# Hybrid decoder step: gate columns projected inside attention, VectorE order in attention and the selection of the late PEER heads rearranged

## What is computed

```python
z = rmsnorm(x, norm_mix) @ w_in              # q, six k/v parts, nsa gates, ssm input u, 2048 merge gates g_mrg
o = gates_cmp*attn_cmp + gates_sel*attn_sel + gates_win*attn_win     # 8 heads of 64, prompt: causal over <=512 keys
y = s5_scan(u)                               # diagonal complex state space, 2048 states
m = sigmoid(g_mrg[:, :1024]) * (o @ w_att_proj) + sigmoid(g_mrg[:, 1024:]) * glu(gelu(y) @ w_ssm_glu)
x = x + m @ w_out
# PEER: 8 heads, 2 x 128 product keys, top 16 of each half, top 16 of the 256 sums
v1, i1 = top_k(q1 @ k1.T, 16); v2, i2 = top_k(q2 @ k2.T, 16); sc, ci = top_k(v1 + v2, 16); e = i1*128 + i2
x = x + sum_hk softmax(sc) * gelu(u_tab[e] . h) * v_tab[e]           # 128 experts for each token
```

## Time and profile before

| | us |
|---|---|
| median of 3 runs | 2407.54 |
| profiled execution, its own time | 2404.02 |
| its span | 2402.3 |
| TensorE busy in the span | 1781.3 (74%) |
| VectorE busy | 1387.7 (58%) |
| GpSimd busy | 685.8 (29%) |
| ScalarE busy | 300.2 (12%) |
| mean granted TensorE clock | 0.772 |
| bytes moved by DMA | 653.88 MB, 562.07 MB of them by GpSimd's gathers |

### The profile page before, as it was taken

How to read it: one execution, slowest core, us unless ns; L and a number is a source line. 1 busy time by engine, 2 the same in 40 slices (tenths; PEclk the granted TensorE clock), 3 DMA queues, 4 the chain that set the end, 5 groups by cost and what they waited for, 6 DMA issues and landing times.

```text
span 2402.3 us, 22802 instructions
## 1 busy us (share of the span) xinstructions
PE 1781.3 (74%) x7910; PEld 814.7 (34%) x7910; DVE 1387.7 (58%) x3448; ACT 300.2 (12%) x686; POOL 685.8 (29%) x828
## 2 busy tenths in 40 slices
PE   7998859997779873888876678656666666666666
PEld 6444746653348561544431334201101011101111
DVE  3899214541132174788645576796577744677644
ACT  3000212220110120222111110000000000000000
POOL 4920100005210202332333222333333333333331
PEclk9899958997999995998986687756665656665557
DMA  4011450005333327999999799899999999999996
GB/s 161 0 50 41 106 157 1 1 1 153 95 103 132 126 79 272 420 414 410 411 414 411 292 382 362 331 359 410 415 416 421 404 415 412 413 410 407 416 413 256
DMA packets 129743, 653.88 MB, mean 272 GB/s; under 512 B 22068, under 2 KB 37092, under 8 KB 59932
## 3 DMA queue, kind: packets, MB, share of 16 engines
q0 software_dynamic: 80000, 562.07, 58.5%
q1 hardware_dynamic: 49628, 90.34, 10.8%
HBM read 645.29 MB, written 11.26 MB: 273 GB/s over the span
## 4 chain that ended last, share of the span: by engine, by line
DMA 22%; PE 17%; DVE 12%; issue 8%; POOL 3%; ACT 0%; DVEq 0%; POOLq 0%; SPq 0%; ACTq 0%
DMA ex_uv<-in_peer_uv,idxT 21%; PE ex_acc L2039 9%; DVE ex_uv L2160 4%; PE ex_hb L1942 3%; POOL ex_uv L1835 3%; DVE ch_iu L1531 1%; PE ex_late L1964 1%; DVE ch_v L1528 1%; PE ex_pick L1992 1%; DVE ch_ci L1531 1%; PE ex_pick L2023 1%; DVE ch_sc L1528 1%; PE ex_late L1992 1%; DVE ch_s L1535 1%; PE ex_late L1979 1%
## 5 line engine op out<-in xcount | busy, mean ns | idle before, releaser
L2160 DVE SCALAR_TENSOR_TENSOR ex_uv<-ex_uv,ex_hb 128x1024 f32<-128x1024 f32 x520 | 628.4, 1219 | 415.8 <-DMA ex_uv<-in_peer_uv,idxT 318.9
L1835 POOL DMA_INDIRECT ex_uv<-in_peer_uv,idxT x520 | 493.0, 948 | 1027.5 <-PE ex_acc L2039 836.3
L1942 PE MATMUL ex_hb<-ex_h_rows,spread 24*128 24x512 bf16 x1040 | 355.8, 505 | 440.3 <-DVE ex_uv L2160 416.8
L2039 PE MATMUL ex_acc<-ex_uv,wts 128*32 128x512 f32 x2080 | 437.3, 963 | 0.0
L1942 PEld LDWEIGHTS ex_hb<-ex_h_rows,spread 24*128 24x128 bf16 x1040 | 52.9, 99 | 775.2 <-DVE ex_uv L2160 629.0
L2275 ACT ACTIVATE ex_gelu<-ex_dots 128x4 f32<-128x4 f32 x130 | 26.7, 205 | 1118.2 <-DVE ex_uv L2160 1116.0
L2039 PEld LDWEIGHTS ex_acc<-ex_uv,wts 128*32 128x32 f32 x2080 | 76.0, 149 | 260.3 <-issue 260.3
L515 PE MATMUL pz<-pr_hT,pr_ring 128*128 128x256 f32 x320 | 71.2, 382 | 0.3 <-ACT hx L443 0.3
L1015 POOL MEMSET de_qbd<- 128x576 f32 x1 | 0.6, 577 | 231.5 <-POOLq L99 231.5
L515 PEld LDWEIGHTS pz<-pr_hT,pr_ring 128*128 128x128 f32 x320 | 60.6, 191 | 10.3 <-issue 1.2
L1528 DVE MAX8 ch_v<-ch_s 128x8 f32<-128x128 f32 x128 | 31.1, 285 | 56.0 <-ACT ch_s L2247 50.6
(11 more groups left out here) (449 smaller groups left out, 2431.6 us busy)
## 6 DMA issues: line engine op xcount, KB each, us to landing
ex_ring<-in_late_w SPq DMA_DIRECT2D x24, 1024.0 KB
pr_ring<-in_w_in SPq DMA_DIRECT2D x6, 2048.0 KB, 8.1
ex_uv<-in_peer_uv,idxT POOLq DMA_INDIRECT x520
w_q<-in_peer_w_q SPq DMA_DIRECT2D x8, 1024.0 KB, 7.7
w_out<-in_w_out SPq DMA_DIRECT2D x2, 2048.0 KB, 17.4
ex_h_rows<-h_split SPq DMA_DIRECT2D x65, 48.0 KB
pr_x<-in_x_prompt SPq DMA_DIRECT2D x4, 512.0 KB, 5.1
pr_ring<-in_w_in_heads SPq DMA_DIRECT2D x1, 2048.0 KB, 10.4
```

Of the source, the lines that this page charges most:

```text
L1835: pool.indirect_dma_start(uv[:, s % SLOTS].rearrange("p j n -> p (j n)"), None, table, bass.IndirectOffsetOnAxis(ap=S.idxT[:, t:t + 1], ax ...
L1942: last = pe.matmul(hb[s % 2][:, CHUNK * h:CHUNK * h + CHUNK], spread[p, k % LOAD, :], h_rows[p, l % 2, CHUNK * h:CHUNK * h + CHUNK], start ...
L2039: last = pe.matmul(acc[LANE * g:LANE * g + LANE, CHUNK * h:CHUNK * h + CHUNK], wts[:, s % (2 * BATCH), LANE - 1 - r:2 * LANE - 1 - r], uv[ ...
L2160: dve.scalar_tensor_tensor(out=rows_, in0=rows_, scalar=1.0, in1=hb[s % 2][:], op0=ALU.mult, op1=ALU.mult, accum_out=dots[:, B % 2, c:c + ...
```

## The change

1. Of the four g chunks only the first stays in `stage_project`; the PE loop runs max(19, 21) = 21 steps, the gelu of the ssm output comes after all groups, cos and sin are loaded right behind the last ring load, and chunks 1 and 2 are loaded into the ring for later (`load_gates`). `hT` and the ring outlive the stage.
2. In `stage_attend` the 12 other groups run: 8 behind the q and k transposes, 2 while VectorE does the compressed softmax, 1 in each of query tiles 0 and 2 of the compressed products. Their sigmoids are on ScalarE (`keep_gates`). SyncE loads chunk 3 between the `w1` loads and the other compression weights, after 4 groups are done.
3. In the units `maxima` is split into `mask` and `maxima`. For i of 2 and 3 the copy L758 comes between them, and the first `keep_busy` is left out.
4. In `stage_experts` the late half-heads are selected in batch j + 33, for late tiles 0 and 2 (tile 2 and the samples); the scores of late tile 1 (tile 3) are kept in `s3` and selected at b = 1 to 16 of tile 2. The splits into thirds are 6 batches apart instead of 3, with `store_rows` ahead of the piece loads. `CHOOSE_LATE` goes from 16 to 17, the exchange of the choice from b = 26 to 27 for n > 0.

```diff
@@ stage_project
-        chunks += [(NAT + 512 + CHUNK * j, CHUNK, "g") for j in range(4)]
+        chunks += [(NAT + 512, CHUNK, "g")]
...
             sp.dma_start(sin, io["rope_sin"]).then_inc(E["tables"], 16)
+            load_gates(sp, io, S, 1, E["z_done"], ends[3])
...
+            load_gates(sp, io, S, 2, E["z_done"], ends[4])
...
-            for j in range(FIRST, len(groups)):
-                s = j - FIRST
+            for s in range(max(len(groups) - FIRST, len(steps) + 5)):
...
-                project(j)
+                if FIRST + s < len(groups):
+                    project(FIRST + s)
+
+def load_gates(sp, io, S, c, done, count):
+    src = io["w_in"].rearrange("a (k p) n -> p (a k) n", p=P)
+    sp.wait_ge(done, count)
+    c0 = NAT + CHUNK + CHUNK * c
+    sp.dma_start(S.ring[:, c % 2], src[:, :, c0:c0 + CHUNK]).then_inc(S.gate_w[c % 2], 16)
@@ stage_attend, SyncE
                     sp.dma_start(S.w1[HD * g:HD * g + HD, j], io[src].rearrange("a s d h -> d (a s) h")).then_inc(E["w_cmp"], 16)
+            load_gates(sp, io, S, 3, E["g_done"], 4)
@@ VectorE
-            def maxima(u):
+            def mask(u):
...
+            def maxima(u):
...
                 if u + 1 < len(UNITS):
-                    maxima(u + 1)
+                    mask(u + 1)
+                    if i < 2:
+                        maxima(u + 1)
...
                 dve.tensor_copy(probT[:, b, 1, 0:P * i + P], tp[:, 1, 0:P * i + P]).then_inc(E["pt1"], 1)
+                if i >= 2 and u + 1 < len(UNITS):
+                    maxima(u + 1)
@@ ScalarE
+            def keep_gates(n, bank):
+                act.wait_ge(E["g_done"], n + 1)
+                act.activation(S.sgT[:, 4 + n, :], bank[:, 0:EARLY_TOK], ACT.Sigmoid).then_inc(E["g_kept"], 1)
...
             act.activation(pc[:], pc[:], ACT.Exp).then_inc(E["cexp_ready"], 1)
+            for n in (8, 9):
+                keep_gates(n, tp[:, n - 8, :])
@@ TensorE
+            def gates_of(n, bank):
...
+            for n in range(8):
+                if n >= 4:
+                    pe.wait_ge(E["g_kept"], n - 3)
+                gates_of(n, sc[:, n % 4, :])
...
+            for n in (8, 9):
+                gates_of(n, tp[:, n - 8, :])
+            pe.wait_ge(E["g_kept"], 10)
             pe.wait_ge(E["coefc_ready"], 1)
...
+                if i % 2 == 0:
+                    gates_of(10 + i // 2, sc[:, i // 2, :])
                 pe.wait_ge(E["ct_kept"], i + 1)
...
-                keep_busy(tp[:, 0, :])
+                if i < 2:
+                    keep_busy(tp[:, 0, :])
@@ stage_experts
-        CHOOSE_LATE = QUERY_AT + HH + 1 - LANE
+        CHOOSE_LATE = QUERY_AT + HH + 2 - LANE
...
-            return B - QUERY_AT - 1 if 0 <= B - QUERY_AT - 1 < HH else None
+            return B - QUERY_AT - 2 if 0 <= B - QUERY_AT - 2 < HH else None
...
+                for t in range(LATE):
+                    if B == TURN_AT + 6 * t + 3:
+                        store_rows(t)
                 for p in range(2, PIECES):
...
-                for t in range(LATE):
-                    if B == TURN_AT + 3 * t + 3:
-                        store_rows(t)
...
-                    dve.wait_ge(E["s_kept"], hh + 1)
-                    best16(dve, link, [(R.v[:, EARLY + t, hh, :], R.iu[:, EARLY + t, hh, :], s2[:, hh % 2, t, :])
-                                       for t in range(TILES - EARLY)])
+                    dve.wait_ge(E["s_kept"], 2 * hh + 2)
+                    best16(dve, link, [(R.v[:, t, hh, :], R.iu[:, t, hh, :], s2[:, hh % 2, t // 2 - 1, :])
+                                       for t in (2, 4)])
...
+                if n == 2 and 1 <= b <= HH:
+                    best16(dve, link, [(R.v[:, 3, b - 1, :], R.iu[:, 3, b - 1, :], s3[:, b - 1, :])])
...
-                t, step = divmod(B - TURN_AT, 3)
+                t, step = divmod(B - TURN_AT, 6)
```

More of the change, by code:

```diff
@@ L476, in _ @@
                 keep(j)
-                if j == GELU_AT:
-                    for k in range(8):
-                        hf, u = divmod(k, 4)
-                        part = S.uT[:, u, SPAN * hf:SPAN * hf + SPAN]
-                        act.wait_ge(E["y_ready"], k + 1)
-                        act.activation(part, part, ACT.Gelu_apprx_tanh).then_inc(E["gelu_done"], 1)
-                    act.wait_ge(E["hs_kept"], 1)
-                    act.activation(S.uT[:, :, SEQ:TOK], y[:, 1, 0:4 * NB].rearrange("p (u b) -> p u b", b=NB),
-                                   ACT.Gelu_apprx_tanh).then_inc(E["gelu_done"], 1)
+            for k in range(8):
+                hf, u = divmod(k, 4)
+                part = S.uT[:, u, SPAN * hf:SPAN * hf + SPAN]
+                act.wait_ge(E["y_ready"], k + 1)
+                act.activation(part, part, ACT.Gelu_apprx_tanh).then_inc(E["gelu_done"], 1)
+            act.wait_ge(E["hs_kept"], 1)
+            act.activation(S.uT[:, :, SEQ:TOK], y[:, 1, 0:4 * NB].rearrange("p (u b) -> p u b", b=NB),
+                           ACT.Gelu_apprx_tanh).then_inc(E["gelu_done"], 1)
         @block.tensor
@@ L746, in maxima @@
                 link(dve.tensor_tensor(diag, diag, causal[:].unsqueeze(1).broadcast_to([P, 2, P]), ALU.add))
+            def maxima(u):
+                i, h = UNITS[u]
+                b = u % 2
                 link(dve.tensor_reduce(nmax[:, b, :], sc[:, 2 * b:2 * b + 2, 0:P * i + P], AX_X, ALU.max))
                 dve.tensor_scalar(nmax[:, b, :], nmax[:, b, :], -1.0, None, ALU.mult).then_inc(E["max_ready"], 1)
+            mask(0)
             maxima(0)
@@ L848, in _ @@
                 last.then_inc(E["tr_done"], 1)
+            def gates_of(n, bank):
+                c, m = divmod(n, 4)
+                c += 1
+                if m == 0:
+                    pe.wait_ge(S.gate_w[c % 2], 16 * (c // 2 + c % 2))
+                for k in range(KT):
+                    last = pe.matmul(bank[:, 0:EARLY_TOK], S.ring[:, c % 2, k, P * m:P * m + P], S.hT[:, k, :],
+                                     start=(k == 0), stop=(k == KT - 1))
+                last.then_inc(E["g_done"], 1)
+            for n in range(8):
+                if n >= 4:
+                    pe.wait_ge(E["g_kept"], n - 3)
+                gates_of(n, sc[:, n % 4, :])
             pe.wait_ge(E["tr_kept"], 2 * TILES)
@@ L867, in _ @@
             pe.wait_ge(E["cmp_kept"], 3)
+            pe.wait_ge(E["g_kept"], 8)
             for i in range(NQ):
@@ L1797, in stage_experts @@
         HH = 2 * HEADS_P
-        CHOOSE, TURN, KEEP = 3, 26, 27
-        CHOOSE_LATE = QUERY_AT + HH + 1 - LANE
+        CHOOSE = 3
+        CHOOSE_LATE = QUERY_AT + HH + 2 - LANE
+        TURN = [26 if n == 0 else 27 for n in range(TILES)]
         EXP = [CHOOSE_LATE + HEADS_P if n == 1 else CHOOSE + HH for n in range(TILES)]
@@ L2054, in _ @@
                 late_work(B, 1)
-                if n < TILES - 1 and b == TURN:
+                if n < TILES - 1 and b == TURN[n]:
                     pe.wait_ge(E["eg_ready"], n + 1)
@@ L2285, in _ @@
                     act.activation(R.eg[:, 1, :], R.eg[:, 1, :], ACT.Exp).then_inc(E["exped"], 1)
-                if n < TILES - 1 and b == KEEP:
+                if n < TILES - 1 and b == TURN[n] + 1:
                     act.wait_ge(E["eg_done"], n + 1)
@@ L2306, in build @@
                                          for n, k in (("merge", 2), ("out", 2), ("route", 4)))
+        S.gate_w = [ctx.enter_context(nc.semaphore(f"gate_w{j}")) for j in range(2)]
         S.out_gain, S.route_keys = (ctx.enter_context(nc.semaphore(n)) for n in ("out_gain", "route_keys"))
```

32 lines of the change are left out of this document (21 added, 11 removed).

## The result

The changed kernel takes 2337.05 us (median of 4 runs, 2333.22 to 2341.23), the kernel before 2407.37 on the same chip: a ratio of 0.9706, 95% interval 0.9685 to 0.9727. The profiled execution has a span of 2331.5 us against 2402.3, 70.8 less. The sum is where it was forecast; its terms are not.

A forecast was written before the change was run, and what follows sets the result against it. Bounds: a chain of waits in attention's front, TensorE's work in the units, DMA in tile 2, VectorE and store waits in tile 1. Terms sum to -70.1 us, 2404.0 to 2333.9, at the median's place 2337; range 2320 to 2360.

The forecast's parts named there:

- Projection, -28.2: End of the projection: twelve gate groups leave, rope starts near 242 instead of 267.9, attention starts about 28.2 us earlier.
- the small product then follows at once, near 241: End of the projection: with twelve groups gone, VectorE gets the small product near 241 and starts rope near 242.
- Front, +13.3: Front of attention: the moved gate groups partly fill TensorE's waits and lengthen the stretch by 13.3 us, bounds +8 and +20.
- Units, -15.4: Attention units: 16 units of i = 2 and 3 lose 0.96 us each with the first dummy, bounds -10 and -15.4.
- the products start on time: Units: VectorE's copy, now ahead of the maxima, ends by T + 1.8, before the second dummy ends at T + 1.9.
- Tile 1, -41.8: Experts, tile 1: selection and store waits go, transfers bound; 354.3 us against 396.1, bounds -50 and -30.
- The row of 28.05 us: Experts, tile 1: SyncE's queue stood 28 us in two piece loads, holding the store ScalarE awaited for 13.04 us.
- Tile 2, +2: Experts, tile 2: sixteen one-row selections of 1.84 us just fit under the transfers; 2 us for unevenness, bounds 0 and +14.
- The front gives more back: Rival, front of attention: four later groups on a cold array cost 13.8 us more, 2351 in all; chance 0.13.
- VectorE bound in tile 2: Rival, experts' tile 2: the added selection is not hidden at all, +27 us, 2364 in all; chance 0.10.
- The clock falls in the units: Rival, units: without the first dummy they run at 1.2 GHz, 83 us more, 2420 in all; chance 0.04.
- The chain in tile 1 stays: Rival, experts' tile 1: scores still awaited in their own batch, 21 us less gain, 2358 in all; chance 0.03.

The follow-up runs named there:

- gates_late: Changed kernel with gate groups 10 and 11 behind the four steps of the compressed products instead of within two of them: 2342.92 us, ratio 0.9743 to the kernel before.
- front_warm: Changed kernel with four dummy matmuls in TensorE's waits in the front of attention: 2328.53 us, ratio 0.9685 to the kernel before.
- only_two_behind: Kernel before with only the selection two batches behind its query, three rows and stores as before: 2376.49 us, ratio 0.9889.

## Why the prediction was right, point by point

**Bound of each stretch: right.** A chain in the front, TensorE's list in the units, VectorE's wait and the store in tile 1, transfers in tile 2. The experiments take the first three out one by one and find their prices; for tile 2 there is the DMA share of 1.01 in both kernels, with 209 and with 235 us of VectorE's work.

**Projection, -28.2: 4.0 too much.** The failed step is "the small product then follows at once, near 241". Twelve groups left, but four of the first chunk stay, and when the state is ready TensorE has the end of one group and the whole of the last still ahead of the product. The order of the instructions showed that before the run. With the product ahead of the last group (`small_first`) rope starts at 242.7, the forecast's place within 0.7.

**Front, +13.3: 7.9 too much, outside its bounds of +8 to +20.** Part of it held: hidden matmuls 35.9 us into the stage (38.4 forecast), no weight late, two groups beside the softmax at +1.2 (1.3 forecast). The largest failed term is the clock in the four steps. Groups 10 and 11 were to cost 4.7 less 2; the four steps took 26.4 us with them against 27.3 without, -0.9 for +2.7. Next is the start-up, put 2.5 too high: of the 4.3 us added for a cold start and a table load 1.8 came (transposes until 8.2 us into the stage, not 6.5, groups 27.7 and not 27.6). The hidden matmuls gave 2 back and not 1, and the piece up to the compressed scores 0.5. `gates_late` and `front_warm` show why: a step cost 6.62 us because its matmuls ran at the lower of the clock's two levels, 1.2 GHz, and both fillings that were tried, gate groups and dummies, paid for themselves. The lower bound +8 assumed full clock in the products and did not take what it gives: 1.91 to 1.06 and 3.67 to 1.99.

**Units, -15.4: 2.5 too much.** The failed step is "the products start on time". The copy arrives at T + 1.87, the products start at T + 2.02, so the copy is the bound of that piece. It was 1.91 before, so a unit loses 0.96 - 0.11 = 0.85 us. The last unit gained nothing (its transposes come 4.84 us after those before it, 4.64 in the kernel before); the forecast gave all sixteen the full gain. That the order is what makes the dummy removable is shown: 3.4 us without it, 12.9 with.

**Tile 1, -41.8: 3.4 too much.** The choice for tile 2 ran at 369 GB/s for 68.7 us, a loss of 68.7 x (1 - 369/413) = 7.3 us (8.1 forecast). The failed step is that this was the only loss in the sum. A second one stands from 1327 to 1370: the rate is 370, 43 x (1 - 370/413) = 4.5 us, where the second late tile's state is split and VectorE waits 3.83 us for ScalarE. That wait alone does not explain it, since the third tile's split has the same 3.83 us at 1404.87 in a stretch (1398 to 1434) that moves 419 GB/s. What delays the gathers stays open.

One reading of the forecast was loose here. The row of 28.05 us joins two piece loads whose issues take 0.36 us each, at 1329.13 and 1356.83; between them SyncE waited for a query of TensorE. The store went out at 1357.23, and ScalarE's 13.04 us are the time until it landed (1370.27); in `only_two_behind` they are 1349.81 to 1363.48. So a store needs some 13 us there, and what the change gives it is time.

**Tile 2, +2: it took 0.1.** The one-row selections, 26 us of VectorE's work (235, not 209), were hidden whole.

**Rivals.** The front gives more back: fell (5.4 us, clock 0.86). VectorE bound in tile 2: fell. The clock falls in the units: fell, even without both dummies. The chain in tile 1 stays: fell. By the Trainium skill's rule (TensorE: Matmul & The Clock Gate, "A second HAM failure mode: psum-queue depth-cycling") short idles between groups of matmuls can make the clock swing. In the units it does not (0.93 us idle in 5.9, clock 0.98). In the compressed products the trace agrees in part: with waits of 1.10 us the clock was at 0.50 throughout before the change, moved between the levels after it, and was at 0.97 once all waits were filled. The forecast weighed the rule for the units and not for the front.

That the total met the forecast to 0.1 us is luck, closer than its own runs lie to each other (2333 to 2341): +4.0, -7.9, +2.5, -1.2, +3.4, -1.9 and +0.4 nearly cancel.
